# Fused two-block transformer on one core: score copies, exponentials, modulation steps and the last norm's weights change their place

## The chip, the cores and the metric

The kernel runs on one core of a Trainium2 chip. The time is the device time of one execution in microseconds (us). The engines are TensorE (PE in the profile, its weight loads PEld), VectorE (DVE), ScalarE (ACT), GpSimd (POOL) and the sync engine (SP), whose queue issues the DMAs. Each engine works through its own instructions in order and waits for the others on semaphores.

## The reference, cut to what matters

A sequence of 256 tokens of width 1024 goes through two blocks in fp32.

```python
def first_block(x, ...):                 # two layers
    h = x + pool_mixer(rms_norm(x, g0), ...)        # projections, window means, group matmul, silu gate
    h = h + hgrn2_mixer(rms_norm(h, g1), ...)       # 16 heads: gated recurrence over chunks of 64
    return rms_norm(h, final_g)

def hgrn2_mixer(h, w_in, lb, norm_g, w_out):
    q, fz, i, gate = split(h @ w_in, 4)             # 4 x 2048 columns
    log_f = logaddexp(log(lb), log1p(-lb) + log_sigmoid(fz)); k = (1 - lb) * sigmoid(-fz)
    o = scan: S_t = diag(f_t) S_{t-1} + k_t v_t^T,  o_t = S_t^T q_t
    o = o * rsqrt(mean(o * o) + EPS) * norm_g       # per head
    return (o * silu(gate)) @ w_out

def second_block(x, c, ctx, ...):
    mod = split(silu(c) @ ada_w + ada_b, 6)         # shifts, gains, gates of both halves
    h = rmsnorm(x) * (1 + mod[1]) + mod[0];  z = h @ w_in;  (the context likewise)
    att = softmax(q k^T + bias, q k_ctx^T) @ [v, v_ctx]        # 8 heads of 64
    y = concat(att, gelu gating, gated convolution of 31 taps) @ w_out
    x = x + mod[2] * y
    h2 = rmsnorm(x) * (1 + mod[4]) + mod[3]
    x = x + mod[5] * conv_ffn(h2)                   # 2 x 2816 up, 3 taps, silu, 2816 down
    return rmsnorm(x) * final_norm_g
```

## The kernel before, in words

**Weights.** All large weights stream through SBUF in units of 128x2048 fp32 (1 MB). `load` on SP brings a unit into one of five `raw` buffers, `hi` on ScalarE (L414) copies it into one of four `w_hi` buffers in rounded fp32, and `lo` on VectorE (L421) computes the remainder `w_lo = raw - w_hi` in place of `raw`. Each product is then three matmuls: high by high, high by low, low by high (L448 to L450 with the weights stationary, `project`; L477 to L479 with the activations stationary, `project_tokens`). Where an engine's program calls `hi(v + RING)` or `lo(v + RING)` is written out by hand, and that place is the place of the copy in the engine's queue. `complete` waits for an output tile in one of four PSUM banks `acc`; `freed` gives the bank back with the instruction that read it.

**Recurrence** (`pe_hgrn`, `act_hgrn`, `dve_hgrn`). It runs over eight pairs of heads, p = 0 to 7. For each pair TensorE projects the query (two tiles, one a head), the forget gate (two tiles) and a wide tile of values (even p) or gates (odd p). ScalarE copies the query tiles (L1386), turns the forget tiles into sigmoids, keys and decays (L1401 to L1408, which end in the signal "factors"), and VectorE builds from them products for seven levels (`levels`, L1331 to L1341). One pair later TensorE multiplies these into scores (`pe_scores_of(p - 1, h)`, L1178 to L1188, head h = 0 between the query and forget tiles, head 1 behind the forget tiles), VectorE copies most of them under masks (`dve_scores_of`, L1199 and L1207), and ScalarE copies the rest (`act_scores_of`, L1219 six times and L1221, signal "exact"). TensorE's scores of the next head wait for "exact" of this one, as they share the banks. The value matmuls (`pe_values_of`) follow after the first half of the wide tile, then squares and gate on ScalarE and VectorE. In pairs 3, 5 and 7 the finished heads of four are scaled by their root (`act_scale_of`, eight ScalarE instructions, L1275), turned by TensorE (`pe_turn_heads`, L1290) and split into high and low (`act_heads_high`, `dve_heads_low`). In pairs 2, 4 and 6, where the variable `q` is None, ScalarE's copies of head 0's scores stand between the gates of the two forget tiles; in pairs 3, 5 and 7 they stand ahead of the forget tiles.

**Second block's input** (`pe_in2` and its partners). The last of its projections are the four query tiles; ScalarE copies them into `QT` (L1780). After the third TensorE computes the scores of attention step 0. A unit of `w_out` is loaded on VectorE behind "gated2" (L1871).

**Attention** runs over eight steps s (four head pairs by two halves of the tokens). For each: `pe_scores` (L1897, two heads e); `dve_softmax` (bias added in PSUM, L1982, negated maximum, L1984); `act_exp` (L1946, into `EE`); `dve_normalize` (reciprocal and scale of `EE`, L1989 and L1992); `pe_turn_e` (eight transposes, L1907); `act_turned` (L1955); every second step `pe_values` (L1918), `act_finish` (L1962) and `dve_finish` (L1998). `EE` has four buffers on top of `XH` and `XL`. Beside them TensorE works on the modulation: `pe_ada` (L864) is one step of `silu(c) @ ada_w`, 8 instructions with 32 stationary columns, from 1 MB of weights loaded by `ada_load`; steps 8 to 15 give one group of rows, 16 to 19 and 20 to 23 the other two. `ADA_BESIDE` lists the steps that stand beside each attention step. VectorE's `lo` of three `w_out` units stands in the loop behind steps 1, 4 and 6, ScalarE's `hi` in steps 2 and 4.

**Output, second norm and end.** `pe_out2_part(half, c, ks)` is a part of the output tile of 128 tokens (half) and 512 columns (c). Modulation steps 20 and 21 stand ahead of the last tile (1, 1), steps 22 and 23 behind it, ahead of the transposes of the normed second half (`pe_turn`, L587). VectorE adds each tile to `x_tok` (L2115, L2118), ScalarE squares it and takes the root, VectorE applies gain and shift (L565, L571). In the feed-forward part the down projection gathers in four PSUM banks `misc`. `dve_end` scales each of its four tiles by the gate row (L2260), adds it to `x_tok` (L2262); ScalarE squares (L531) and takes the root (L548); behind the last tile VectorE takes the reciprocals (L554) and multiplies `x_tok` by root and weights (L565), and SP stores it.

## Time and profile before

| | us |
|---|---|
| median of 3 runs (848.02 to 849.5) | 848.49 |
| profiled execution | 849.81 |
| its span, first to last instruction | 848.6 |
| TensorE busy | 819.3 (97%) |
| VectorE busy | 592.6 (70%) |
| ScalarE busy | 460.5 (54%) |
| GpSimd busy | 48.1 (6%) |
| TensorE's mean granted clock | 0.993 of full speed |

A busy time is an average over stages: the recurrence lies between about 197 and 447 us of the span, the second block's projections between 480 and 578, attention between 578 and 615, output and norm between 615 and 651, feed-forward from there to 842. Idle time of an engine that is not the bound costs nothing, so a row tells little until it is placed in its stage. In a timeline the first number is the start, the second the duration; the bracket is the idle time of the engine before the row and what ended it.

### The profile page before, as it was taken

To read this page: it belongs to the slowest core of one execution; us is meant where nothing else is said; L and a number is where in the kernel's file an instruction comes from. 1 tells how busy PE (TensorE), PEld (TensorE's weight loads), DVE (VectorE), ACT (ScalarE), POOL (GpSimd) and SP (SyncE) were. 2 spreads that over 40 slices of the span, in tenths; PEclk is the share of its full clock that TensorE was granted. 3 is DMA by queue.
4 is the path that set the end of the run, shared out by engine and by line. 5 is a ranking of instruction groups with operands and counts; after the bars stand their busy time and mean duration, and the time that the engine had idled before them with its cause. 6 is when DMAs were issued, how large, how long until landed. Compare 5 with 4: busy or idle time off the path is not lost.

```text
span 848.6 us, 13159 instructions
## 1 busy us (share of the span) xinstructions
PE 819.3 (97%) x5363; PEld 714.4 (84%) x5363; DVE 592.6 (70%) x843; ACT 460.5 (54%) x764; POOL 48.1 (6%) x67
## 2 busy tenths in 40 slices
PE   9999999999998998998999999997998999999996
PEld 7998988878997997997988789884466999999995
DVE  6765455646799798798785886897928765666564
ACT  6645444445577857857756552555635544444432
POOL 8100002600000000000000000000000000000000
PEclk9999999999999999999999999999998999999998
DMA  8879875783643443445346763845536455556531
GB/s 286 300 256 242 242 248 199 234 297 118 196 142 107 150 149 108 141 149 188 111 157 234 272 236 131 317 150 194 183 143 222 150 198 192 168 187 199 187 111 49
DMA packets 102631, 160.07 MB, mean 189 GB/s; under 512 B 11318, under 2 KB 67994, under 8 KB 100267
## 3 DMA queue, kind: packets, MB, share of 16 engines
q1 hardware_dynamic: 102570, 159.24, 57.1%
q8 instruction: 42, 0.69, 0.3%
q14 instruction: 19, 0.15, 0.1%
HBM read 156.02 MB, written 3.21 MB: 188 GB/s over the span
## 4 chain that ended last, share of the span: by engine, by line
PE 85%; DVE 7%; ACT 4%; DMA 3%; issue 2%; POOL 0%; POOLq 0%; DVEq 0%
PE acc L448 12%; PE acc L450 12%; PE acc L449 12%; PE acc L477 9%; PE acc L479 9%; PE acc L478 9%; PE misc L1185 2%; PE misc L2169 2%; PE misc L2167 2%; PE misc L2168 2%; PE misc L864 1%; PE misc L587 1%; DMA raw<-in_w_in_dram 1%; DVE soft L1984 1%; PE misc L1290 1%
## 5 line engine op out<-in xcount | busy, mean ns | idle before, releaser
L421 DVE TENSOR_TENSOR w_lo<-raw,w_hi 128x2048 fp32r<-128x2048 f32 x114 | 263.4, 2320 | 105.6 <-ACT w_hi L414 105.6
L414 ACT ACTIVATE w_hi<-raw 128x2048 fp32r<-128x2048 f32 x114 | 217.4, 1911 | 109.3 <-PE acc L450 26.6
L448 PE MATMUL acc<-XH,w_hi 128*128 128x256 f32 x848 | 242.8, 286 | 0.0
L449 PE MATMUL acc<-XL,w_hi 128*128 128x256 f32 x848 | 240.9, 284 | 0.0
L450 PE MATMUL acc<-XH,w_lo 128*128 128x256 f32 x848 | 240.8, 284 | 0.0
L448 PEld LDWEIGHTS acc<-XH,w_hi 128*128 128x128 f32 x848 | 163.1, 192 | 4.2 <-issue 1.8
L449 PEld LDWEIGHTS acc<-XL,w_hi 128*128 128x128 f32 x848 | 163.2, 192 | 0.8
L450 PEld LDWEIGHTS acc<-XH,w_lo 128*128 128x128 f32 x848 | 163.0, 192 | 0.0
L477 PE MATMUL acc<-w_hi,XH 128*128 128x512 f32 (+1 forms) x224 | 87.4, 390 | 0.8 <-DVE w_lo L421 0.8
L479 PE MATMUL acc<-w_hi,XL 128*128 128x512 f32 (+1 forms) x224 | 85.6, 382 | 0.0
L478 PE MATMUL acc<-w_lo,XH 128*128 128x512 f32 (+1 forms) x224 | 85.6, 382 | 0.0
L477 PEld LDWEIGHTS acc<-w_hi,XH 128*128 128x128 f32 x224 | 42.2, 188 | 9.3 <-DVE w_lo L421 1.0
L479 PEld LDWEIGHTS acc<-w_hi,XL 128*128 128x128 f32 x224 | 42.1, 188 | 8.4
L478 PEld LDWEIGHTS acc<-w_lo,XH 128*128 128x128 f32 x224 | 42.2, 188 | 7.4
L1331 DVE TENSOR_TENSOR KQ<-QK,DD 128x512 f32<-128x512 f32 x56 | 38.7, 691 | 5.2 <-ACT DB L1408 3.5
L2169 PE MATMUL misc<-w_hi,FL 128*128 128x512 f32 x88 | 34.6, 393 | 0.0
L2167 PE MATMUL misc<-w_hi,FH 128*128 128x512 f32 x88 | 34.4, 391 | 0.0
L2168 PE MATMUL misc<-w_lo,FH 128*128 128x512 f32 x88 | 34.3, 390 | 0.0
L1335 DVE TENSOR_TENSOR DD<-DD,DB 128x512 f32<-128x512 f32 x48 | 32.9, 685 | 0.0
L1207 DVE COPY_PREDICATED AT<-mask_level,misc 128x128 f32<-128x128 uint8 x80 | 28.7, 358 | 2.7
L1219 ACT ACTIVATE AT<-misc 32x32 f32<-32x32 f32 (+1 forms) x96 | 18.9, 197 | 19.6 <-DVE AT L1207 18.7
L2193 ACT ACTIVATE GP<-acc 128x256 f32<-128x256 f32 x22 | 8.5, 386 | 35.7 <-PE acc L450 34.7
(280 smaller groups left out, 1333.5 us busy)
## 6 DMA issues: line engine op xcount, KB each, us to landing
raw<-in_hgrn_w_in_dram SPq DMA_DIRECT2D x32, 1024.0 KB, 5.7
ada_raw<-in_ada_w_dram SPq DMA_DIRECT2D x24, 1024.0 KB, 7.2
raw<-in_ffn_w_up_dram SPq DMA_DIRECT2D x22, 1024.0 KB, 5.1
raw<-in_pool_w_in_dram SPq DMA_DIRECT2D x15, 1024.0 KB, 6.0
raw<-in_ffn_w_down_dram SPq DMA_DIRECT2D x11, 1024.0 KB, 4.8
raw<-in_w_in_dram SPq DMA_DIRECT2D x10, 1024.0 KB, 7.2
raw<-in_pool_w_out_dram SPq DMA_DIRECT2D x8, 1024.0 KB, 5.2
raw<-in_hgrn_w_out_dram SPq DMA_DIRECT2D x8, 1024.0 KB, 5.0
```

The lines of the kernel that those rows point to most:

```text
L414: self.hi_done.up(act.activation(self.w_hi[v % RING][:, 0:w], self.raw[j][:, 0:w], ACT.Copy), v)
L421: self.lo_done.up(dve.tensor_tensor(self.w_lo[j][:, 0:w], self.raw[j][:, 0:w], self.w_hi[v % RING][:, 0:w].bitcast(F32), ALU.subtract), v)
L448: pe.matmul(o, wh[:, k, c:c + P], xh[:, k, :], start=k == 0, stop=False)
L449: pe.matmul(o, wh[:, k, c:c + P], xl[:, k, :], start=False, stop=False)
L450: m = pe.matmul(o, wl[:, k, c:c + P], xh[:, k, :], start=False, stop=k == K - 1)
L477: pe.matmul(o, x, wh[:, k, c:c + width], start=first and k == 0, stop=False)
L478: pe.matmul(o, x, wl[:, k, c:c + width], start=False, stop=False)
L479: m = pe.matmul(o, y, wh[:, k, c:c + width], start=False, stop=end)
L1331: n = V.up(dve.tensor_tensor(o, src, dec, ALU.mult), "levels", p)
L2167: pe.matmul(o, xh[:, k, ts], wh[:, k, f], start=i == 0 and k == 0, stop=False)
L2168: pe.matmul(o, xh[:, k, ts], wl[:, k, f], start=False, stop=False)
L2169: m = pe.matmul(o, xl[:, k, ts], wh[:, k, f], start=False, stop=i == 10 and k == 1)
```

## The change

Four parts. (1) In the recurrence ScalarE copies head 0's scores of pairs 2, 4 and 6 ahead of the forget tiles, and in pairs 3, 5 and 7 scales the finished heads between the two query copies. (2) The exponentials of attention step 0 are computed behind the third query tile, into `EE` buffers at another address (the old one lies under the projection's activations), after ScalarE's copy of a weight unit that stood in the loop; VectorE normalises step 0 ahead of the loop, one of its three weight remainders moves ahead of attention, two behind the last normalisation, and one modulation step goes ahead of attention. (3) Modulation steps 20 and 21 go behind the last output tile. (4) In the last norm VectorE multiplies each tile by the weights as soon as it is summed, finishes the first half ahead of the second half's tiles, and the final scaling is shared: VectorE columns 0 to 511, ScalarE columns 512 to 1023.

```diff
--- before.py
+++ after.py
@@ -212,7 +212,8 @@
 
         self.ada_raw += [at(kb, f"ada_raw{3 + n}", [UNIT]) for n, kb in enumerate((74, 82, 90, 48, 24))]
 
-        self.EE = [self.at(x_at + 2 * n * K, f"EE{n}", [512]) for n in range(4)]
+        self.EE = [at(44 + 2 * n, f"EE{n}", [512]) for n in range(2)]
+        self.EE += [self.at(x_at + 2 * n * K, f"EE{2 + n}", [512]) for n in range(2)]
         self.PT = [self.at(x_at + (8 + 4 * n) * K, f"PT{n}", [4, TOK]) for n in range(2)]
         self.PT += [at(90 + 4 * n, f"PT{2 + n}", [4, TOK]) for n in range(2)]
         self.m_row = at(56, "m_row", [D])
@@ -1382,14 +1383,15 @@
             if p > 1:
                 act.wait_ge(self.T.h, self.T["scored", p - 2, 1])
             for h in range(2):
+                if h and q is not None:
+                    self.act_scale_of(q)
                 b = self.complete(act, query, h)
                 self.freed(query, h, act.activation(self.queries_of(QK, h), acc[b][:, 0:TOK].rearrange("p (a t) -> p a t", a=2),
                                                     ACT.Copy))
-            if q is not None:
-                self.act_scale_of(q)
             self.hi(self.first(query) + RING)
             if q is not None:
                 self.act_heads_high(q, 0)
+            if p > 1:
                 self.act_scores_of(p - 1, 0)
             if p:
                 act.wait_ge(self.V.h, self.V["levels", p - 1])
@@ -1407,8 +1409,8 @@
                 act.activation(self.queries_of(self.DD, h), decay, ACT.Identity, bias=l0, scale=l1)
                 A.up(act.activation(self.DB[0][:, h * TOK:h * TOK + TOK], self.sigma[:, 1, :], ACT.Identity, bias=l0,
                                     scale=l1), "factors", p, h)
-                if p and q is None and h == 0:
-                    self.act_scores_of(p - 1, 0)
+                if p == 1 and h == 0:
+                    self.act_scores_of(0, 0)
             self.hi(self.first(forget) + RING)
             if q is not None:
                 self.act_heads_high(q, 1)
@@ -1788,6 +1790,8 @@
             if n == 2:
                 act.wait_ge(self.V.h, self.V["gated2"])
                 A.up(act.activation(self.MIXH[:, 4:6, :], self.U[:, :, :], ACT.Copy), "mix_gate")
+                self.hi(self.first(q, 0) + RING)
+                self.act_exp(0)
 
     def conv_taps(self, k0, k1):
         dve, V, u = self.nc.vector, self.V, self.u_cv
@@ -1869,7 +1873,8 @@
         t = V.up(dve.tensor_tensor(mv, mv, view(self.BS, 0, (P, 2), (0, 2), (1, P)), ALU.add))
         dve.wait_ge(V.h, t)
         V.up(dve.tensor_tensor(uv, uv, mv, ALU.mult), "gated2")
-        self.lo(self.first(v, 0) + RING)
+        for n in range(2):
+            self.lo(self.first(v, n) + RING)
 
     def dve_mix(self, name, k, src):
         dve = self.nc.vector
@@ -1880,7 +1885,7 @@
 
 
 
-    ADA_BESIDE = ((12, 13), (14,), (15,), (16,), (17,), (18,), (19,), ())
+    ADA_BESIDE = ((13,), (14,), (15,), (16,), (17,), (18,), (19,), ())
     STEPS = NA_HEADS
 
     def score_bank(self, s, e):
@@ -1922,6 +1927,7 @@
 
     def pe_attention(self):
         pe = self.nc.tensor
+        self.pe_ada(12)
         for n in range(4):
             self.wait_freed(pe, self.u_q, n)
             self.wait_freed(pe, self.u_v, n)
@@ -1962,14 +1968,12 @@
         self.A.up(act.activation(self.MIXH[:, j, :], self.acc[b][:, 0:TOK], ACT.Copy), "mix", j)
 
     def act_attention(self):
-        for s in range(self.STEPS):
+        for s in range(1, self.STEPS):
             self.act_exp(s)
-            if s:
-                self.act_turned(s - 1)
+            self.act_turned(s - 1)
             if s > 2 and s % 2:
                 self.act_finish(s // 2 - 1)
-            if s in (2, 4):
-                self.hi(self.first(self.u_q, s // 2 - 1) + RING)
+        self.hi(self.first(self.u_q, 1) + RING)
         self.act_turned(self.STEPS - 1)
         self.act_finish(3)
 
@@ -2002,20 +2006,21 @@
         dve, V, v = self.nc.vector, self.V, self.first(self.u_out2)
         dve.wait_ge(self.bias_back.h, self.bias_back["all"])
         self.dve_softmax(0)
-        for s in range(self.STEPS):
+        self.dve_normalize(0)
+        self.dve_softmax(1)
+        self.dve_mix("mix_conv", 6, self.CA)
+        self.dve_mix("mix_gate", 4, self.U)
+        for s in range(1, self.STEPS):
             if s + 1 < self.STEPS:
                 self.dve_softmax(s + 1)
             if s == 3:
                 self.dve_ada(1)
             self.dve_normalize(s)
-            if s == 0:
-                self.dve_mix("mix_conv", 6, self.CA)
-                self.dve_mix("mix_gate", 4, self.U)
             if s > 2 and s % 2:
                 self.dve_finish(s // 2 - 1)
-            if s in (1, 4, 6):
-                self.lo(v + (1, 4, 6).index(s) + 1)
         self.dve_ada(2)
+        for n in range(2, 4):
+            self.lo(v + n)
         self.dve_finish(3)
 
 
@@ -2068,14 +2073,12 @@
         pe.wait_ge(self.A.h, self.A["shift", "ffn"])
         self.pe_last_rows("ffn_gain", 2, (0, 1))
         self.pe_out2_part(1, 0, (4, 5, 6, 7, 0, 1, 2, 3))
-        self.pe_ada(2 * KD + 4)
-        self.pe_ada(2 * KD + 5)
         self.pe_out2_part(1, 1, (4, 5, 6, 7))
         for c in range(2):
             self.pe_turn("ffn", 0, c, self.XN3)
         self.pe_out2_part(1, 1, (0, 1, 2, 3))
-        self.pe_ada(2 * KD + 6)
-        self.pe_ada(2 * KD + 7)
+        for a in range(2 * KD + 4, 3 * KD):
+            self.pe_ada(a)
         for c in range(2):
             self.pe_turn("ffn", 1, c, self.XN3)
 
@@ -2249,30 +2252,36 @@
                 act.wait_ge(self.V.h, self.V["last", half, c])
                 self.act_square("end", half, self.x_tok[:, half, c * 512:c * 512 + 512], self.XN3[:, half, c * 512:c * 512 + 512], c)
             self.act_root("end", half, 2)
+            act.wait_ge(self.V.h, self.V["rstd", "end", half])
+            y = self.Y[:, half, 512:D]
+            self.A.up(act.activation(y, y, ACT.Copy, scale=self.nstat[:, half, 4:5]), "scaled", "end", half)
 
     def dve_end(self):
+
         dve, V = self.nc.vector, self.V
         dve.wait_ge(self.gain_in["end"].h, self.gain_in["end"]["all"])
         for half in range(2):
             for c in range(2):
                 f = slice(c * 512, c * 512 + 512)
+                x, y = self.x_tok[:, half, f], self.Y[:, half, f]
                 dve.wait_ge(self.T.h, self.T["down", half, c])
-                t = V.up(dve.tensor_tensor(self.Y[:, half, f], self.misc[2 * half + c][:, :], self.e_row[:, f], ALU.mult))
+                t = V.up(dve.tensor_tensor(y, self.misc[2 * half + c][:, :], self.e_row[:, f], ALU.mult))
                 dve.wait_ge(V.h, t)
-                V.up(dve.tensor_tensor(self.x_tok[:, half, f], self.Y[:, half, f], self.x_tok[:, half, f], ALU.add),
-                     "last", half, c)
+                t = V.up(dve.tensor_tensor(x, y, x, ALU.add), "last", half, c)
+                dve.wait_ge(V.h, t)
+                V.up(dve.tensor_tensor(y, x, self.last_row[:, f], ALU.mult))
             self.dve_part("end", half)
-        for half in range(2):
             self.dve_root("end", half)
-            self.dve_scale("end", half, self.x_tok, self.x_tok, self.last_row)
+            y = self.Y[:, half, 0:512]
+            V.up(dve.tensor_scalar(y, y, self.nstat[:, half, 4:5], None, ALU.mult), "scaled", "end", half)
 
     def sp_end(self):
         sp = self.nc.sync
         for half in range(2):
             for c in range(2):
-                f = slice(c * 512, c * 512 + 512)
-                sp.wait_ge(self.V.h, self.V["scaled", "end", half, c])
-                self.stored.up(sp.dma_start(self.out[0, half * P:half * P + P, f], self.x_tok[:, half, f]), "all", by=16)
+                f, by = slice(c * 512, c * 512 + 512), (self.V, self.A)[c]
+                sp.wait_ge(by.h, by["scaled", "end", half])
+                self.stored.up(sp.dma_start(self.out[0, half * P:half * P + P, f], self.Y[:, half, f]), "all", by=16)
         sp.wait_ge(self.stored.h, self.stored["all"])
```

## Rows read from the trace of the kernel before

**Rows 1.** Waits of TensorE: engine, line, whom for; total us, times, longest us.
```profile
PE misc L1178 <- ACT AT L1221: 6.7, 3, 2.2
PE misc L1907 <- DVE EE L1992: 5.8, 5, 2.2
PE misc L587 <- DVE XN L571: 3.4, 2, 2.7
PE misc L1290 <- ACT SG L1275: 1.7, 3, 0.6
```
**Rows 2.** Timelines of pair 4: VectorE, ScalarE, TensorE (start us, us, engine, line, operation).
```profile
315.39 1.93 DVE L1207 COPY_PREDICATED AT<-mask_level,misc 128x128 f32<-128x128 uint8 x5
...
337.78 0.69 DVE L1341 TENSOR_TENSOR KQ<-QK,DD 128x512 f32<-128x512 f32 x1
...
317.81 1.28 ACT L1401 ACT_TABLE_LOAD   x1 [2.96 <-issue]
...
322.86 0.68 PE L1178 MATMUL misc<-QK 128*128 128x128 f32 x4 [2.25 <-ACT AT L1221]
...
330.63 0.38 PE L1236 MATMUL misc<-VT,AT 128*128 128x128 f32 x2
...
343.20 0.60 PE L1178 MATMUL misc<-QK 128*128 128x128 f32 x4
```
**Rows 3.** Timelines of pair 2: VectorE, ScalarE, TensorE.
```profile
256.08 1.94 DVE L1207 COPY_PREDICATED AT<-mask_level,misc 128x128 f32<-128x128 uint8 x5
...
256.19 1.28 ACT L1401 ACT_TABLE_LOAD   x1 [3.82 <-issue]
257.49 0.39 ACT L1401 ACTIVATE sigma<-acc 128x256 f32<-128x256 f32 x1
...
259.58 1.23 ACT L1219 ACTIVATE AT<-misc 32x32 f32<-32x32 f32 x6
260.83 0.28 ACT L1221 ACTIVATE AT<-misc 128x128 f32<-128x128 f32 x1
...
269.02 0.38 PE L1236 MATMUL misc<-VT,AT 128*128 128x128 f32 x2
```
**Rows 4.** Timelines of pair 5: ScalarE, TensorE.
```profile
343.39 0.38 ACT L1386 ACTIVATE QK<-acc 128x256 f32<-128x256 f32 x1 [2.44 <-PE acc L450]
343.67 2.43 ACT L1275 ACTIVATE SG<-SG,hstat 128x128 f32<-128x128 f32 x8
...
346.16 1.05 PE L1290 MATMUL misc<-ident,SG 128*128 128x128 f32 x7 [0.56 <-ACT SG L1275]
```
**Rows 5.** Timelines of attention: VectorE, TensorE.
```profile
580.40 0.43 DVE L1982 TENSOR_TENSOR acc<-acc,BIAS 128x256 f32<-128x256 f32 x1 [2.56 <-PE acc L1897]
...
587.06 0.88 DVE L1992 TENSOR_SCALAR EE<-EE,soft 128x512 f32<-128x512 f32 x2
587.86 2.29 DVE L421 TENSOR_TENSOR w_lo<-raw,w_hi 128x2048 fp32r<-128x2048 f32 x1
...
613.56 1.09 PE L1907 MATMUL misc<-ident,EE 128*128 128x128 f32 x8
```
**Rows 6.** Timelines of output and second norm: ScalarE, TensorE.
```profile
640.96 1.92 ACT L414 ACTIVATE w_hi<-raw 128x2048 fp32r<-128x2048 f32 x1 [2.54 <-DMA raw<-in_ffn_w_up_dram]
...
644.20 1.92 PE L864 MATMUL misc<-ada_raw,s_pad 128*32 128x512 f32 x16
```
**Rows 7.** Windows of 1 us: PE, PEld, DVE, ACT, POOL busy, granted clock, DMA share, GB/s.
```profile
649.00:650.00 1.00, 0.59 (x4) 0.27 (x3) 0.97 (x2) 0.37 (x1) 0.00 (x0) 0.65 0.80 233
...
656.00:657.00 1.00, 1.00 (x10) 1.00 (x10) 0.94 (x3) 0.36 (x1) 0.00 (x0) 0.94 0.00 0
```
**Rows 8.** Timeline of VectorE at the end.
```profile
837.90 0.69 DVE L2260 TENSOR_TENSOR Y<-misc,e_row 128x512 f32<-128x512 f32 x1 [5.02 <-PE misc L2169]
...
842.68 0.69 DVE L2262 TENSOR_TENSOR x_tok<-Y,x_tok 128x512 f32<-128x512 f32 x1
...
845.06 1.42 DVE L565 SCALAR_TENSOR_TENSOR x_tok<-x_tok,nstat,last_row 128x512 f32<-128x512 f32 x2
```

## The prediction

> **What bounds the kernel now.** I read the page first: TensorE is busy 97% of the span. Such a kernel gets shorter only where TensorE stands still, where its clock is low, or in the tail after its last matmul. So the second view was TensorE's waits [rows 1]: 6.7 us on the score copies in three places, 5.8 us on the normalised exponentials, 3.4 us on the rows of the last modulation, 1.7 us on the scaled heads. Then came the timelines of the three engines around each wait [rows 2 to 6], the granted clock [rows 7], and the tail [rows 8]. VectorE is far from idle in these stages, so each moved step was placed in its queue.
>
> **Score copies (pairs 2, 4, 6).** In pair 4 VectorE ends the masked copies at 317.3; ScalarE is then idle for 2.96 us until the forget tile is there, loads a table, computes head 0's gates and only then copies the scores, and TensorE stands 2.25 us [rows 2]. With the copies first, ScalarE copies in the idle time: 1.23 + 0.28 = 1.5 us [rows 3], 317.3 to 318.9. TensorE would be free at 322.86 - 2.25 = 320.6, so the whole 2.25 goes. Queued behind the copies: the table load and both heads' gates. They start at 318.9 instead of 317.8, but no copies lie between the heads, so the second head's factors come 0.4 earlier. Next is the second head's exact scores, before the value matmuls: 327.9 on ScalarE against a TensorE that arrives at 330.63 - 2.25 = 328.4, 0.5 us to spare. The level products end at 337.8 + 0.7 and are read at 343.2, nearly 5 us of slack [rows 2]. Pair 6 repeats pair 4: 4.5 us for both.
>
> Pair 2 differs: VectorE has weight remainders queued ahead, and its masked copies end only at 258.0 [rows 3]. ScalarE, free since 252.4, would now wait for them while forget tile 0 has been ready since 256.2. Copies end at 259.6, the gates follow at 259.7 and end at 265.1, 2.0 later than now; with a 1.9 us weight copy and 1.5 us of copies behind them the second exact scores are there at 268.5. TensorE gets there at 269.02 - 1.5 = 267.5 and waits a microsecond. Of the 2.25 only 0.4 is left: a new wait takes the place of the old one.
>
> The Trainium skill, "ScalarE: Activation LUTs", section "What ACT_TABLE_LOAD costs", says that each switch of tables costs a drain besides the load, 2.66 us together. By that page the gates behind the copies would come 1.4 us later again, and the copies' gain would be some 3 us less. In pair 2 the load takes 1.28 us and the sigmoid starts 0.02 behind it [rows 3]; by the trace the drain isn't there.
>
> **Head scaling (pairs 3, 5, 7).** The 2.43 us of scaling start when the second query copy is done, and TensorE waits 0.56 for them [rows 4]. Put ahead of that copy they run in 2.44 us in which ScalarE idles. All three waits (1.7) go, since the reciprocals they read are ready by then; the second query copy moves by at most 0.3 and nobody is near it. Recurrence: 0.4 + 4.5 + 1.7 = 6.6 gained. Ends: 5.0, if the margin of 0.5 is eaten in pairs 4 and 6 and a scaling wait stays; 8.4, if pair 2 gives all of its wait.
>
> **Exponentials, attention.** VectorE sets the pace here: per head pair two maxima with bias adds (2.14) and one normalisation (1.0), and between them three weight remainders of 2.2 each, two of them on the chain of work that ended last [rows 5]. The change takes these out of the loop. The one moved forward fills idle time (VectorE idles before the first softmax until 575.6). The two moved back stand behind the last normalisation, ahead of the last output remainder; I get 616.3 for the second, and its first reader on TensorE is at 619.3 in the new timing: hidden by 3 us. ScalarE's weight copy, ahead of the first exponential, runs from 575.4 to 577.3, and its data landed before; the exponential ends at 578.75, so the last query copy, queued behind it, is 0.15 late. TensorE's first modulation step (1.0) covers that gap but puts the second scores 0.3 later. Normalising pair 0 in VectorE's 2.56 us of idleness takes 1.0 out of the chain.
>
> Played through step by step with these durations TensorE starts the second transposes at 586.8, the third at 590.0, the seventh at 606.4 and the last at 610.4, against 613.56 now [rows 5]. So 3.2 are gained, not 6.6: once the remainders are gone TensorE's own scores, modulation steps and value matmuls are the bound in the middle. Ends: 2.0, if hand-overs each cost 0.1 more; 4.5, if no wait stayed.
>
> **Modulation steps behind the last output tile.** Two steps, 1.92 us [rows 6], move. The second half's rows don't come earlier for it. Their chain starts with a weight load issued when the first column's second half is done (635.8), lands at 640.96, and goes through ScalarE's weight copy, XH, XL and the add [rows 6]; none of that depends on the moved steps. TensorE reaches the first half's transposes 1.9 earlier and now waits there (0.35 and 0.9), and its later wait shrinks from 2.7 [rows 1] to about 1.3: same sum, in smaller pieces. Time from order alone: 0, up to 0.3 either way. The bias loads and the final weights' load behind the last step are issued 1.3 later, with over 100 us to spare.
>
> What may change is the clock. After that 2.7 us stall TensorE's granted clock is 0.50, its lower level of 1.2 GHz, from about 649.65 to 656.06 [rows 7]; at 2.4 GHz the matmuls of these 6.4 us would have been through 2.8 us sooner, waits taken out. In attention TensorE stood still 2.2 us at a stretch [rows 1] and the clock stayed at 1.00. With no stall above 1.4 us I take it that the clock stays up: 2.8 gained. Ends: 0 and 2.9. The Trainium skill, "TensorE: Matmul & The Clock Gate", section "What's actually happening", says that recent activity, not one wait, decides. By that page the narrow steps and transposes between short stalls need not keep the clock up; this is the first rival.
>
> **The last norm.** VectorE works without a pause from 837.9 to the last sum (842.68 + 0.6) [rows 8], though TensorE ends only at 841.9. The change adds a multiply by the weights (0.69) to each of four tiles, three of them ahead of the last sum: +2.1. It also puts the first half's finish in the queue: wait for ScalarE's root 0.5, reciprocal 0.2, scaling 0.5 (a 512-wide one is 0.44 in [rows 5]): +1.2. The last sum comes 3.3 later. Behind it: square, accumulator read and root end 1.2 after the sum in both; now 0.4 of waiting, 0.2 and 1.42 follow, later 0.25 and one scaling of 0.6 on each engine: 1.1 less. The stores are 2.1 either way. Loss 2.2. Ends: 1.2 and 3.0.
>
> **Sum** against the profiled execution (849.81, span 848.6, 1.2 outside): -6.6 - 3.2 - 2.8 + 2.2 = -10.4, hence 839.4. The median of the three runs is 848.49, 1.3 below that execution; the forecast for the median is 838.1.
>
> **Rivals.**
> - The clock falls all the same. For: the stall only splits, the sum of idleness around the transposes is unchanged. Against: 2.2 us stalls among narrow matmuls kept the clock in attention. 838.1 + 2.8 = 840.9.
> - Less comes back in recurrence and attention: both at their lower ends (+1.6, +1.2), with the clock low as well, 843.7; without it 840.9. For: the 0.5 us margin in pairs 4 and 6.
> - The tail is free: if VectorE's extra multiplies fitted beside the matmuls, the last sum wouldn't move and 1.1 would be gained: 838.1 - 3.3 = 834.8. Against it: no pause in [rows 8].
> - Slower: the recurrence turns from TensorE-bound into a loop of dependent steps. Level products (10.8), scores 2.2, masked copies 2.3, copies 1.5, table and gates 5.5 make 22.3 us a pair, against a period of 30.8 now. If every weight copy and remainder queued there (11.1) lay in that loop, the period would be 33.4, 2.6 more for each of six pairs, instead of 6.6 saved: 838.1 + 6.6 + 15.6 = 860.3. It decides from a loop of 30.8; the 5 us of slack in [rows 2] speak against it.
> - The change doesn't do what it says: something late by as much in the next stage eats it, 848.5. The chain of work that ended last runs over TensorE between these stages, against it.
>
> **How the numbers follow.** Forecast 0.45, clock low 0.24, less comes back 0.14, tail free 0.10, eaten 0.04, slower 0.03. The range reaches from the free tail to the second rival without its worst: 834.8 to 843.2. A measurement of this kernel can tell 0.2%, 1.7 us, from no change. Faster 0.93, same 0.04, slower 0.03.
>
> **What would show it.** TensorE's wait on the score copies gone in pairs 4 and 6, one of about 1 us before the value matmuls of pair 2; the wait on the scaled heads gone; the last attention transposes 3 us closer to the last query tile; two short stalls at the first half's transposes and a granted clock of 1.00 behind them; the last sum 3 us further from the last matmul. I am wrong if the second exact scores are late in pair 4, or if VectorE's queue in the tail is shorter than counted.

## The result and the profile after

The changed kernel takes 839.21 us (median of 4 runs, 837.09 to 839.93) against 848.94 for the kernel before (848.02 to 849.5): ratio 0.9873, 95% interval 0.9847 to 0.9899 (dividing the two medians gives 0.9885, inside that interval). Faster, 1.1 us above the forecast and within the range. Timed again beside later experiments it took 839.98 against 847.67, ratio 0.9902 (0.9884 to 0.992). The profiled execution took 838.5, its span is 837.2 against 848.6.

TensorE's waits after (columns as in [rows 1]):

```profile
PE misc L1912 <- DVE EE L1996: 2.9, 2, 2.0
PE misc L588 <- DVE XN L572: 2.7, 3, 1.7
...
PE misc L588 <- DVE nstat L540: 0.7, 1, 0.7
PE misc L1179 <- ACT AT L1222: 0.7, 1, 0.7
...
PE misc L1237 <- ACT AT L1222: 0.3, 1, 0.3
```

The score copies' 6.7 us in three waits are 0.7 in one, with a new wait of 0.3 before pair 2's value matmuls; the scaled heads' 1.7 is gone, and the normalised exponentials' 5.8 is 2.9. The rows of the last modulation still cost 3.4 (2.7 + 0.7), in four pieces instead of two:

```profile
625.80 0.66 PE L588 MATMUL misc<-ident,XN 128*128 128x128 f32 x4 [0.35 <-DVE XN L572]
627.19 0.66 PE L588 MATMUL misc<-ident,XN 128*128 128x128 f32 x4 [0.73 <-DVE nstat L540]
...
635.83 0.66 PE L588 MATMUL misc<-ident,XN 128*128 128x128 f32 x4 [1.66 <-DVE XN L572]
637.22 0.95 PE L588 MATMUL misc<-ident,XN 128*128 128x128 f32 x4 [0.73 <-DVE XN L572]
```

Waits don't add up to a time. A ledger does: the distances between points of the timelines that both kernels have. The stages are: start to the second group of transposes of the first norm in this part (A), from there to the last scores of the recurrence (recurrence), to the first attention scores (B), to the last attention transposes (attention), to the second gate copy of the first unit behind the second norm (second norm), to the first product of the tail (units), to the end of the span (tail).

| us | A | recurrence | B | attention | second norm | units | tail |
|---|---|---|---|---|---|---|---|
| before | 192.32 | 250.85 | 131.19 | 39.20 | 45.77 | 178.57 | 10.7 |
| after | 189.85 | 242.43 | 131.07 | 37.09 | 44.84 | 178.56 | 13.4 |
| after, second trace | 191.75 | 242.44 | 130.96 | 36.98 | 44.70 | 178.57 | 13.4 |

Stage A holds nothing of the change, and it alone differs by 2.5 us between the first two traces: that much of the profiled 11.4 isn't the change's. What is: recurrence -8.4, attention -2.1, second norm -0.9, tail +2.7; together -8.7.

Where pair 4's second scores waited 2.25 us, TensorE's timeline has no wait in its brackets:

```profile
308.19 0.60 PE L1179 MATMUL misc<-QK 128*128 128x128 f32 x4
...
316.18 0.60 PE L1179 MATMUL misc<-QK 128*128 128x128 f32 x4
```

and ScalarE's shows the copies (L1220, L1222) ahead of the table load:

```profile
313.07 1.25 ACT L1220 ACTIVATE AT<-misc 32x32 f32<-32x32 f32 x6 [2.50 <-DVE AT L1208]
314.33 0.28 ACT L1222 ACTIVATE AT<-misc 128x128 f32<-128x128 f32 x1
314.62 1.28 ACT L1403 ACT_TABLE_LOAD   x1
315.92 0.38 ACT L1403 ACTIVATE sigma<-acc 128x256 f32<-128x256 f32 x1
```

ScalarE copies as soon as VectorE's masked copies are done, 1.6 us ahead of TensorE's next need at 316.18. The table load starts 0.01 behind the copy and the sigmoid 0.02 behind the load: the drain of the Trainium skill, "ScalarE: Activation LUTs", section "What ACT_TABLE_LOAD costs", named in the prediction, isn't there after the change either.

Attention and the second norm, in windows of 2 us (columns as in [rows 7]):

```profile
574.00:576.00 2.00, 0.14 (x1) 0.14 (x2) 1.93 (x6) 1.53 (x4) 0.00 (x0) 1.00 0.86 295
576.00:578.00 2.00, 2.00 (x12) 1.55 (x15) 1.93 (x5) 0.24 (x2) 0.00 (x0) 0.50 0.48 197
578.00:580.00 2.00, 2.00 (x10) 0.30 (x4) 1.29 (x4) 2.00 (x6) 0.00 (x0) 0.65 0.00 0
...
636.00:638.00 2.00, 1.27 (x9) 0.84 (x8) 1.81 (x3) 0.60 (x1) 0.00 (x0) 0.86 0.99 256
638.00:640.00 2.00, 2.00 (x10) 2.00 (x10) 1.16 (x2) 1.79 (x2) 0.00 (x0) 0.50 0.95 391
640.00:642.00 2.00, 2.00 (x16) 2.00 (x15) 2.00 (x2) 2.00 (x2) 0.00 (x0) 0.79 0.10 39
```

The granted clock is at its lower level (0.50, 1.2 GHz) for 3.4 us behind the stop ahead of the second attention transposes, where it had stayed at 1.00, and for 3.4 us in the second norm, where it had been low for 6.8.

The tail, VectorE and ScalarE:

```profile
823.84 0.69 DVE L2268 TENSOR_TENSOR Y<-misc,e_row 128x512 f32<-128x512 f32 x1 [5.02 <-PE misc L2172]
...
831.90 0.69 DVE L2270 TENSOR_TENSOR x_tok<-Y,x_tok 128x512 f32<-128x512 f32 x1
...
834.00 0.72 ACT L2257 ACTIVATE Y<-Y,nstat 128x512 f32<-128x512 f32 x1 [0.23 <-DVE nstat L555]
834.00 0.49 DVE L2276 TENSOR_SCALAR Y<-Y,nstat 128x512 f32<-128x512 f32 x1
```

The last sum starts 8.06 us behind the first product; before it was 842.68 - 837.90 = 4.78 [rows 8]. That is 3.3 later, as forecast.

### The profile page after: what moved, and what is told of

It reads as the page before. It is cut to its first block, busy times and chain, and to the rows that moved or that the text cites. A ratio compares the mean times of both kernels' runs of the same rounds, so it can differ in the third digit from the quotient of the medians.

```text
span 837.2 us, 13163 instructions
## 1 busy us (share of the span) xinstructions
PE 816.1 (97%) x5363; PEld 712.2 (85%) x5363; DVE 594.2 (71%) x845; ACT 462.3 (55%) x766; POOL 53.8 (6%) x67
## 4 chain that ended last, share of the span: by engine, by line
PE 87%; DVE 6%; DMA 3%; ACT 3%; issue 1%; SPq 0%; ACTq 0%; DVEq 0%
PE acc L449 13%; PE acc L450 13%; PE acc L451 13%; PE acc L478 9%; PE acc L479 9%; PE acc L480 9%; PE misc L1186 3%; PE misc L2172 2%; PE misc L2170 2%; PE misc L2171 2%; PE misc L865 2%; DMA raw<-in_w_in_dram 1%; PE acc L1923 1%; ACT w_hi L415 1%; DMA raw<-in_hgrn_w_in_dram 1%; PE misc L1291 1%
## 5 line engine op out<-in xcount | busy, mean ns | idle before, releaser
L1220 ACT ACTIVATE AT<-misc 32x32 f32<-32x32 f32 (+1 forms) x96 | 18.9, 197 | 28.7 <-DVE AT L1208 27.8
```

## The experiments

### The parts alone

**The recurrence's part alone**, in the kernel before:

```diff
             for h in range(2):
+                if h and q is not None:
+                    self.act_scale_of(q)
...
-            if q is not None:
-                self.act_scale_of(q)
...
+            if p > 1:
                 self.act_scores_of(p - 1, 0)
...
-                if p and q is None and h == 0:
-                    self.act_scores_of(p - 1, 0)
+                if p == 1 and h == 0:
+                    self.act_scores_of(0, 0)
```

> The kernel before with the recurrence's part of the change alone: score copies ahead of the forget gates, head scaling between the two query copies. The computation is whole. Theory A, the terms as forecast: what goes is what the waits show, 0.4 + 4.5 + 1.7 = 6.6 us faster, with TensorE's wait on the score copies 0.7 in pair 2 and none in pairs 4 and 6. Theory B, read from the two traces: between the first scores of pair 1 and those of the last pair the changed kernel won 8.4, so each removed stop costs more than the idle time that its row shows: 8.4 us faster. Theory C: part of those 8.4 is what two executions differ by anyway; then less than 6.6.

Measured: 840.48 against 848.81, ratio 0.9894 (0.9871 to 0.9916). The ledger's recurrence stage is 242.47, against 250.85: 8.4 less. Theory B holds; theory A's 6.6 would be a ratio of 0.9922, outside the interval. Where the extra 1.8 lie is seen around the scaled heads of pair 5, first in the kernel before, with the row of 346.16 [rows 4] between these two:

```profile
345.21 0.39 PE L1188 MATMUL misc<-KQ 128*128 128x128 f32 x2
...
347.07 0.36 PE L448 MATMUL acc<-XH,w_hi 128*128 128x256 f32 x1
```

and then with the recurrence's part alone:

```profile
339.79 0.39 PE L1188 MATMUL misc<-KQ 128*128 128x128 f32 x2
340.02 1.06 PE L1290 MATMUL misc<-ident,SG 128*128 128x128 f32 x8
340.83 0.36 PE L448 MATMUL acc<-XH,w_hi 128*128 128x256 f32 x1
```

From the last score matmul to the first transpose it was 0.95 us and is 0.23: 0.72 less, where the wait's row said 0.56. A row (0.39) is longer than the distance to the next one (0.23), since matmuls overlap, so the idle time is counted from 0.16 too late. The transposes then took 0.91 to the next matmul and take 0.81. This stop costs its idle row and 0.27 more. In pair 4 the distance between the two heads' scores went from 322.86 - 312.47 = 10.39 to 317.51 - 309.52 = 7.99, 2.40 for a wait of 2.25, and 0.07 more behind it: 0.22 beyond the row. Five stops went entirely, three of 0.27 and two of 0.22: 1.3 of the 1.8. The rest is in pair 2:

```profile
258.54 0.68 PE L1178 MATMUL misc<-QK 128*128 128x128 f32 x4 [0.73 <-ACT AT L1221]
...
266.35 0.38 PE L1236 MATMUL misc<-VT,AT 128*128 128x128 f32 x2
...
267.46 0.49 PE L1236 MATMUL misc<-VT,AT 128*128 128x128 f32 x2 [0.28 <-ACT AT L1221]
```

The copies came when forecast, but head 0's value matmuls (266.35 to 267.0) don't need head 1's exact scores. They run during the wait, and 0.28 of it is left instead of 1.0.

**The attention's part alone** (`EE` buffers 0 and 1 in a place of their own, as in the change; the edit is shown in part):

```diff
+                self.hi(self.first(q, 0) + RING)
+                self.act_exp(0)
...
-    ADA_BESIDE = ((12, 13), (14,), (15,), (16,), (17,), (18,), (19,), ())
+    ADA_BESIDE = ((13,), (14,), (15,), (16,), (17,), (18,), (19,), ())
...
+        self.dve_normalize(0)
+        self.dve_softmax(1)
...
-            if s in (1, 4, 6):
-                self.lo(v + (1, 4, 6).index(s) + 1)
```

> The kernel before with the attention's part alone: two of the score tables in a place of their own, first exponential ahead of the last query tile, remainders out of the loop, one modulation step ahead of the last query tile. The computation is whole. Theory A, as forecast: 3.2 us faster. Theory B, from the changed kernel's trace: TensorE stands 2.0 us ahead of the second transposes, the granted clock falls behind it and gives back some 1.7, so 2.1 or less is left, with a granted clock under 0.9 in the 10 us around the second transposes. In the later stage the stall of 2.7 ahead of the second half's transposes and the low clock behind it stay as they are.

Measured: 845.86 against 848.81, ratio 0.9964 (0.995 to 0.9978), 3.0 less by the medians. The interval reaches from 1.9 to 4.2 us and holds both theories, so the trace has to tell. Attention 37.07, with the granted clock low behind the 2.0 us stop again. But with the recurrence's part alone, whose attention is that of the kernel before, the clock was low there too (0.83 from 580 to 590) and attention took 40.78 instead of 39.20. So the low stretch isn't the new order's alone, and the comparison has to be made at one clock: with one low stretch, 40.78 to 37.07, 3.7 less; at 1.00, 39.20 to 35.51 (in the two kernels with products on GpSimd, below), 3.7 less.

**The modulation steps alone.**

```diff
         self.pe_out2_part(1, 0, (4, 5, 6, 7, 0, 1, 2, 3))
-        self.pe_ada(2 * KD + 4)
-        self.pe_ada(2 * KD + 5)
...
-        self.pe_ada(2 * KD + 6)
-        self.pe_ada(2 * KD + 7)
+        for a in range(2 * KD + 4, 3 * KD):
+            self.pe_ada(a)
```

> The kernel before with the third part alone: modulation steps 20 and 21 behind the last output tile. The computation is whole. Theory A, as forecast: nothing from the order, 2.8 us from a clock that stays up. Theory B, from the changed kernel's trace: the 2.7 us stall splits in pieces, the clock falls all the same but for 4 us instead of 6.4, so about 1.0 faster. Theory C: the order alone costs or gives up to 0.3 and the clock is as before: no difference.

Measured: 848.09 against 848.81, ratio 0.999 (0.9971 to 1.0008): no difference that can be measured, and theory A's 2.8 lies just outside the interval, which ends at 2.5. In its trace the second norm takes 44.73, with one low stretch of 3.4; and the recurrence, all as in the kernel before, takes 252.60 instead of 250.85, since the clock was low there for 3.4 us from about 385.8, behind pair 6's stop of 2.25 us. That stop stands in pairs 2, 4 and 6 of three traces (this one, the kernel before, the attention's part alone), and the clock fell behind one of the nine. A stretch of low clock comes at a place in one trace and not in the next.

**The change with the old end** (ScalarE's share of the scaling and the stores taken back too):

```diff
-                t = V.up(dve.tensor_tensor(x, y, x, ALU.add), "last", half, c)
-                dve.wait_ge(V.h, t)
-                V.up(dve.tensor_tensor(y, x, self.last_row[:, f], ALU.mult))
...
+        for half in range(2):
             self.dve_root("end", half)
-            y = self.Y[:, half, 0:512]
-            V.up(dve.tensor_scalar(y, y, self.nstat[:, half, 4:5], None, ALU.mult), "scaled", "end", half)
+            self.dve_scale("end", half, self.x_tok, self.x_tok, self.last_row)
```

> The changed kernel with the last norm as it was before: weights multiplied in the last scaling on VectorE, no product beside the squares. The computation is whole. Theory A, as forecast: 2.2 us less than the changed kernel, 837.0, last sum 3.3 us closer to the last matmul. Theory B, from the two traces (14.06 us ahead at the first product of the tail, 11.4 at the end): 2.7 less, 836.5. Theory C, the tail was free: 1.1 more than the changed kernel, 840.3.

Measured: 837.4 against 848.81, ratio 0.986 (0.9839 to 0.9882). The tail takes 836.2 - 825.55 = 10.65 us instead of 837.2 - 823.84 = 13.36: 2.7, theory B, and no free tail (theory C). The medians of the two kernels are 1.8 apart, in different comparisons; they don't separate theories A and B.

### What the clock does, and part 3

**The changed kernel again**, as it is:

> The changed kernel once more, unaltered, as the yardstick for the next three kernels and as a second trace. Theory A: its granted clock falls in attention again, one stretch of about 3.4 us, since it fell in all three traces that hold the attention's part; 839.2. Theory B: the low stretches come and go between executions of one program (five of the runs of the kernel before had a mean clock of 0.996, three of 0.989); then this trace may have the attention at full clock, shorter by 1.6 us, 35.5 from first scores to last transposes instead of 37.1.

Its trace is the last row of the ledger: attention 36.98, with the clock low for 3.4 us. Theory A in this execution. Of the kernels below, the two with products on GpSimd are the same up to the last norm, and their traces show theory B.

**The old end, steps 20 and 21 unmoved** (the diff of the modulation steps undone):

> The changed kernel with the old end and with modulation steps 20 and 21 back before the last output tile. The computation is whole. It is compared with the changed kernel with the old end (837.4). Theory A, as forecast: 2.8 us slower, 840.2, for the clock falls for longer. Theory B, from the traces with and without the moved steps: from the last attention transposes to the second gate copy of the first unit it takes 44.3 where the clock is low for 3.4 us and 45.7 where it is low for 6.8, against 44.75 to 44.84 with the steps moved: so 0.4 faster if the low stretch is short and 1.0 slower if it is long. Theory C: no difference that can be measured, 837.4.

Measured: 836.59, ratio 0.9868 (0.9853 to 0.9883), beside 0.986 with the steps moved: no difference that can be measured, and theory A (2.8 slower) is out. Second norm 44.70, one low stretch.

**Step 14 beside the first head pair** (this kernel and the next two have the old end):

```diff
-    ADA_BESIDE = ((13,), (14,), (15,), (16,), (17,), (18,), (19,), ())
+    ADA_BESIDE = ((13, 14), (15,), (16,), (17,), (), (18,), (19,), ())
```

> The changed kernel with the old end, and with modulation step 14 beside the first head pair instead of the second, the later ones spread so that the fifth has none. The computation is whole. TensorE stands 1.99 us ahead of the second transposes and is the bound from there to the seventh. Theory A: the step (1.0) fills half of that stop and no longer lies in TensorE's own chain, 1.0 less: 836.4. Theory B: with no stop of 2 us the granted clock stays at 1.00 in attention as well, another 1.6: 834.8. Theory C: VectorE is the bound behind the fifth pair, and the step taken out there comes back as a wait: 837.4.

Measured: 835.05, ratio 0.9855 (0.9841 to 0.987), near theory B's 834.8, but not for its reason alone. The clock stayed at 1.00, yet attention took 36.61, because of a wait that no theory had:

```profile
576.65 1.09 PE L1912 MATMUL misc<-ident,EE 128*128 128x128 f32 x8 [1.46 <-DVE EE L1996]
582.90 1.06 PE L865 MATMUL misc<-ada_raw,s_pad 128*32 128x512 f32 x8 [2.03 <-DVE ada L878]
```

Step 16 opens a new sum in its bank and waits until VectorE has added up the steps before it, which it does only beside the fourth pair. Moved ahead of that, it stopped TensorE for 2.03 us. In this trace the second norm had no low stretch either (43.54 us), which hides that loss in the time. The mended order keeps step 16 in its place:

```diff
+    ADA_BESIDE = ((13, 14), (15,), (), (16,), (17,), (18,), (19,), ())
```

> The changed kernel with the old end and with step 14 beside the first head pair; step 16 stays beside the fourth, since it waits for the sum of steps 8 to 15, which VectorE adds only there (in the kernel before this one it stood ahead of that and TensorE waited 2.0 us for it). The third pair has no step. The computation is whole. At a granted clock of 1.00 the changed order takes 35.5 us from first scores to last transposes, at one low stretch 37.0 to 37.1. Theory A: step 14 fills half of the 1.99 us stop and leaves TensorE's chain: 34.5, and 1.0 less than the changed kernel with the old end in the median, 836.4. Theory B: VectorE is the bound behind the third pair and the step comes back as a wait: 35.5, 837.4. Theory C: a shorter stop also spares the low stretch: 34.5 with a clock of 1.00, and 834.8 in the median.

Measured: 833.36 against 848.71, ratio 0.9814 (0.9799 to 0.983), 832.22 to 834.6. Attention takes 34.65 us at a clock of 1.00; 34.5 had been expected:

```profile
576.96 1.09 PE L1912 MATMUL misc<-ident,EE 128*128 128x128 f32 x8 [1.46 <-DVE EE L1996]
595.21 1.09 PE L1912 MATMUL misc<-ident,EE 128*128 128x128 f32 x8 [0.90 <-DVE EE L1996]
```

The order gave 0.86, by 35.51 - 34.65. In the four traces with a first stop of 1.46 us the clock never fell in attention; with one of 1.99 it fell in five (36.9 to 37.1 us) and stayed up in two (35.51). The same eight transposes behind the same stop show the two levels, in the changed kernel

```profile
575.86 1.89 PE L1912 MATMUL misc<-ident,EE 128*128 128x128 f32 x8 [1.99 <-DVE EE L1996]
```

and with products on GpSimd:

```profile
577.85 1.09 PE L1912 MATMUL misc<-ident,EE 128*128 128x128 f32 x8 [1.99 <-DVE EE L1996]
```

That speaks for theory C, without settling it: the stop of 2.03 us above, in a kernel with a first stop of 1.46, left the clock up too.

**The mended kernel with steps 20 and 21 unmoved:**

> The mended kernel with the old end, with modulation steps 20 and 21 back before the last output tile, beside the same kernel with them moved. The computation is whole. Theory A, as forecast for the third part: 2.8 us slower, from a clock that stays low for longer. Theory B, from the traces so far: low for 3.4 us in five of the six with the steps moved, for none in one; without the move 3.4 in two, 6.8 in two; order alone 0.1 to 0.4 in favour of the steps unmoved: within 1.0 of the kernel beside it. From last transposes to the second gate copy: 43.5 without a low stretch, 44.3 to 44.8 with one of 3.4, 45.7 with 6.8.

Measured: 835.59 (834.01 to 836.16), ratio 0.9837 (0.9822 to 0.9853), 2.2 above the kernel with them moved on the same chip. Theory B had allowed 1.0, theory A 2.8. The second norm takes 45.80 against 44.98, the clock low for 6.8 us, 0.8 of the 2.2:

```profile
630.00:640.00 10.00, 6.71 (x36) 4.08 (x36) 7.61 (x12) 4.07 (x7) 0.00 (x0) 0.74 0.73 261
640.00:650.00 10.00, 10.00 (x79) 10.00 (x79) 9.89 (x13) 6.62 (x8) 0.00 (x0) 0.92 0.33 102
```

All traces of this stage together: with the steps unmoved 6.8 us low in three (45.64 to 45.80) and 3.4 in two (44.34, 44.70); with them moved 3.4 in eight (44.68 to 45.07) and none in one (43.54). Means 45.25 and 44.70: the part is worth half a microsecond in this stage, by few traces. The three pairs of timings say -0.8, 0.7 and 2.2, and none reaches the forecast's 2.8.

### Another end

**Products on GpSimd** (the changed kernel, with GpSimd's products in place of VectorE's for three of four tiles; scalings shared with ScalarE):

```diff
+            pool.wait_ge(self.V.h, self.V["last", half, c])
+            self.G.up(pool.tensor_tensor(self.Y[:, half, f], self.x_tok[:, half, f], self.last_row[:, f], ALU.mult),
+                      "product", half, c)
```

> The changed kernel with another end: three of the four products with the weights on GpSimd, beside VectorE's sums, the fourth on VectorE behind its last sum, where it waits for the root anyway; scalings shared with ScalarE. The computation is whole. Compared with the changed kernel with the old end (837.4, 10.65 us from the first product of the tail to the end of the span). Theory A: the last sum comes only 0.2 later (one reciprocal), and what lies behind it is 0.75 shorter: 10.1 from first product to end, 836.9. Theory B: GpSimd's products get in VectorE's way, each sum beside them takes longer than its 0.69, or the products are late: 11.5 or more, as with the changed kernel's tail, where the last sum came 3.3 later and the tail took 13.36.

Measured: 836.79, ratio 0.987 (0.9855 to 0.9884). That is theory A's 836.9, by luck: the clock stayed up in attention here (35.51), and the tail takes 836.3 - 824.43 = 11.9 us, theory B:

```profile
825.15 0.69 DVE L2283 TENSOR_TENSOR x_tok<-Y,x_tok 128x512 f32<-128x512 f32 x1
825.76 0.68 DVE L2281 TENSOR_TENSOR Y<-misc,e_row 128x512 f32<-128x512 f32 x1
...
826.00 1.31 POOL L2299 TENSOR_TENSOR Y<-x_tok,last_row 128x512 f32<-128x512 f32 x1 [433.30 <-DVE x_tok L2283]
...
826.48 1.37 DVE L2283 TENSOR_TENSOR x_tok<-Y,x_tok 128x512 f32<-128x512 f32 x1
```

VectorE's sum, two operands in SBUF, takes 1.37 instead of 0.69 beside GpSimd's product and ends 0.5 behind it, and so do the next two sums (1.23 and 1.07); its product, one operand in PSUM, runs beside GpSimd's at 0.68.

**The same with VectorE's first product left in PSUM:**

```diff
-                t = V.up(dve.tensor_tensor(y, self.misc[2 * half + c][:, :], self.e_row[:, f], ALU.mult))
+                m = self.misc[2 * half + c][:, :]
+                t = V.up(dve.tensor_tensor(m, m, self.e_row[:, f], ALU.mult))
                 dve.wait_ge(V.h, t)
-                t = V.up(dve.tensor_tensor(x, y, x, ALU.add), "last", half, c)
+                t = V.up(dve.tensor_tensor(x, m, x, ALU.add), "last", half, c)
```

> The end with three products on GpSimd, where VectorE's three sums beside them took 1.37, 1.23 and 1.07 us instead of 0.69, while its products, which read PSUM, stayed at 0.68 to 0.69. Now VectorE's first product is left in PSUM, so that the sum too reads one operand from there. The computation is whole. Theory A: only operations of VectorE with both operands in SBUF are held up by GpSimd's; then each sum takes 0.69 again, the last sum comes 0.2 later than with the old end, and the tail takes 10.1 us from first product to end instead of 11.9 (old end: 10.65). Theory B: any sum beside a product of GpSimd is held up, or a result in PSUM costs as much: 11.5 or more.

```profile
824.96 3.93 POOL L2300 TENSOR_TENSOR Y<-x_tok,last_row 128x512 f32<-128x512 f32 x3 [432.97 <-DVE x_tok L2284]
...
825.45 0.69 DVE L2284 TENSOR_TENSOR x_tok<-misc,x_tok 128x512 f32<-128x512 f32 x1
...
826.84 0.69 DVE L2284 TENSOR_TENSOR x_tok<-misc,x_tok 128x512 f32<-128x512 f32 x1
```

Measured: 835.2, ratio 0.9837 (0.9823 to 0.9851). Every sum is back at 0.69 under GpSimd's products; the tail takes 833.6 - 823.38 = 10.2 us (10.1 expected, old end 10.65). The Trainium skill, "SBUF — State Buffer", section "Who interferes with whom", says just this: a VectorE instruction with two SBUF inputs contends with a GpSimd one that reads SBUF, one with at most one, outside the perf modes that use two ports, doesn't. Both traces agree.

**Both together**, the mended steps and this end:

> The last two in one kernel: step 14 earlier, and the end with products on GpSimd and VectorE's first product in PSUM. The computation is whole. Stage by stage it should be their sum: 34.5 from first scores to last transposes (36.0 with a low stretch), and 10.1 for the tail if the sums are free of GpSimd, 11.5 or more if not; 0.5 less or 0.9 more than the mended kernel with the old end.

Measured: 834.01 (831.96 to 835.56), ratio 0.9819 (0.98 to 0.9838). By the ledger it is the sum: attention 34.65, tail 10.3 (832.8 - 822.52). Against the mended kernel with the old end (833.36) the 0.4 of the tail is below what such a timing can tell. Either of the two is the fastest version found, 5 to 6 us below the changed kernel's 839.21.

## Why the prediction was right, and where its terms were not

The total came out 1.1 us above the forecast, but through errors of both signs, and that it is so near is partly luck: by the ledger the four parts gave 8.7 together, where the sum had 10.4.

- **Recurrence, 6.6 forecast, 8.4 measured.** The mechanism was right: the waits of pairs 4 and 6 and of the scaled heads are gone, and a wait stands in pair 2 in place of the old one. Two sizes were off. Each stop was priced at its idle row, and costs 0.22 to 0.27 more: 1.3 for five. In pair 2 I took both heads' value matmuls to wait for head 1's exact scores; head 0's don't, so that 0.9 was gained instead of 0.4. The upper end (8.4) covered it.
- **Attention, 3.2 forecast.** The order gives 3.7 at one clock (39.20 to 35.51). Played through, the second transposes lay 12.4 behind the first scores, and they lie 12.5 behind; the last were forecast at 36.0 and come at 35.5. Missing from the forecast is the clock. I had taken it that 2 us stalls leave it up in attention, since they did in the one trace; it fell in five of seven traces with this order and in one of three with the old one, and costs 1.5 to 1.6 each time (37.0 - 35.5, 40.8 - 39.2).
- **Modulation steps, 2.8 forecast, about half a microsecond measured.** The order came as said: TensorE waits 0.35 and 0.73 at the first half's transposes, and the sum of the waits stays 3.4. The step that failed is "with no stall above 1.4 us I take it that the clock stays up". The later stall was 1.66 with 0.73 behind it (1.3 had been forecast), and the clock fell in eight traces of nine, for 3.4 us. This is the rival that the clock falls all the same, for part of the time. The 6.4 us of low clock before the change were read too short as well: a mean of 0.65 over a microsecond, half of it granted when low, means low for 0.7 of it, and the stretch is 6.8 us, 649.3 to 656.1 [rows 7]. At the same clock, one low stretch of 3.4 us, the unmoved order took 44.34 and 44.70 us and the moved one 44.68 to 45.07; two more stops may be the reason, which no run shows.
- **Tail, 2.2 forecast, 2.7 measured.** The last sum is 3.3 later, as summed from VectorE's queue. What follows it is 0.98 shorter, not 1.1, as ScalarE's scaling takes 0.72 instead of 0.6. And the stores are not "2.1 either way": from the last scaling to the end it was 2.12 (848.6 - 846.48) and is 2.48 (837.2 - 834.72). Both halves of the last rows now come ready within 0.3 us of each other, and the last store takes longer: from the last scaling's end it is issued after 0.18 us instead of 0.02 and lands 2.31 behind that instead of 2.05. That the store right ahead of it is the reason is likely, not shown. The rival of a free tail is refuted.
- **The range and the baseline.** The forecast rested on one profiled execution, 1.3 above the median. Stage A, which the change doesn't touch, differs by up to 2.5 us between traces; an error of that size was in the base whatever the terms.

What stays open is what makes the clock fall in one execution and not in another. The traces show the place, around the end of a stop of TensorE (from 0.4 us before it to 1.5 us behind it), and the price, but not the condition; the length of the stop alone isn't it.

## What to carry to other kernels

Price a stop of the bounding engine by the distance between the starts of the instructions around it, less their usual distance, and not by the idle time in its row; here that added some quarter of a microsecond (0.22 to 0.27) for each stop. A part of the gain that rests on the clock staying up is a chance, not a term: look at the same place in several executions before counting on it. Work beside a tail is free only if its engine pauses there, and handing it to an idle engine is free only if that doesn't hold up the busy one (here its sums took 1.07 to 1.37 us instead of 0.69).

## What the runs showed of the chip

- From the start of the recurrence to the last matmul a stretch of low granted clock was 3.4 us long in most cases (6.8 in three traces of 14), and one of 3.4 cost 1.1 to 1.75 us of time by the stages above. Kernels that are the same up to the last norm had it in attention in three traces and not in two: 37.0 to 37.1 and 35.51 us. Among 23 timings of the kernel before, all the same program, five had a mean granted clock of 0.996 (846.99 to 848.08 us) and three one of 0.989 (849.95 to 854.41).
- A product 128x512 on GpSimd from SBUF takes 1.31 us, nearly twice VectorE's 0.69, and holds up a VectorE sum with two SBUF operands: each of three ended 0.5 us behind the product beside it (1.07 to 1.37 instead of 0.69). Leaving the intermediate result in PSUM cost nothing (0.69 to 0.70) and took the conflict away.
- Apart from the clock, two stages repeat from trace to trace within a tenth of a microsecond (recurrence in the new order 242.40 to 242.49 in eleven traces, units 178.56 to 178.57 in all fourteen), the one between recurrence and attention within 0.5 (130.80 to 131.30), while the part up to the recurrence differs by 2.5 (189.85 to 192.32).
